# The router beside the last projection, expert weights through one ring, expert 0's rows put together on TensorE

## What is computed

```
mix = sigmoid(ga) * (o_a @ w_proj_a) + sigmoid(gb) * (o_b @ w_proj_b)
x   = x + mix @ w_out
h   = rms_norm(x, norm_ffn)
g      = argmax(h @ w_router_group + b)                      # one of 4 groups
top2   = top_k((h @ w_router_expert + b)[experts of g], 2)   # two of its 4 experts
weight = softmax(top2 values) * softmax(group logits)[g]
x   = x + sum over the two experts e of weight_e * ((silu(h @ w_gate[e]) * (h @ w_up[e])) @ w_down[e])
y   = rms_norm(x, norm_final)
```

## Time and profile before

| | us |
|---|---|
| Runs | 1137.81, 1140.47, 1141.32 (median 1140.47) |
| Profiled execution | 1137.26, span 1135.3, mean PE clock 0.950 |
| PE busy | 1022.2 (90%) |
| DVE, ACT, POOL busy | 642.3, 540.9, 141.9 |
| pb's last product to wo's first | 685.82 to 689.25 |
| First expert product | 795.97 |
| Last product of the last down projection | 1097.24 |
| First gathered output row added (DVE) | 1111.91 |

### The profile page before, as it was taken

How to read it: one execution, slowest core, us unless ns; L and a number is a source line. 1 busy time by engine, 2 the same in 40 slices (tenths; PEclk the granted TensorE clock), 3 DMA queues, 4 the chain that set the end, 5 groups by cost and what they waited for, 6 DMA issues and landing times.

```text
span 1135.3 us, 17498 instructions
## 1 busy us (share of the span) xinstructions
PE 1022.2 (90%) x7174; PEld 933.4 (82%) x7174; DVE 642.3 (57%) x919; ACT 540.9 (48%) x717; POOL 141.9 (13%) x138
## 2 busy tenths in 40 slices
PE   2999999999999999999899898981799999999940
PEld 2999999998999988888888898971688888888830
DVE  5233731344221267686665464247488988989826
ACT  6215633342222245454645422061478778887722
POOL 3300000000000123332211100022001010110003
PEclk8999999999999999999999999985799999999975
DMA  7863545417465375574434446123689999999726
GB/s 158 259 85 72 55 76 69 82 39 111 73 76 111 62 115 64 72 78 82 151 115 131 147 146 256 51 95 114 204 308 414 414 413 414 413 414 414 272 113 236
DMA packets 125514, 198.01 MB, mean 174 GB/s; under 512 B 10864, under 2 KB 72304, under 8 KB 125440
## 3 DMA queue, kind: packets, MB, share of 16 engines
q1 hardware_dynamic: 112336, 149.37, 49.4%
q0 software_dynamic: 10176, 36.97, 8.9%
q10 hardware_dynamic: 2928, 10.62, 2.3%
HBM read 174.40 MB, written 22.54 MB: 173 GB/s over the span
## 4 chain that ended last, share of the span: by engine, by line
PE 84%; DVE 6%; DMA 4%; ACT 3%; issue 2%; POOL 0%; ACTq 0%; DVEq 0%; POOLq 0%
PE ps L1019 24%; PE ps L1021 23%; PE ps L1020 23%; PE ps L1004 5%; DMA ring<-in_w_in_dram 2%; PE ps L1153 2%; PE ps L1139 2%; DVE x L1767 1%; DVE h_lo L1371 1%; PE ps L1083 1%; PE ps L1115 1%; PE ps L1099 1%; PE ps L1114 1%; DVE fo L1762 1%; DMA yg<-y_rows,ysl 1%
## 5 line engine op out<-in xcount | busy, mean ns | idle before, releaser
L1704 DVE TENSOR_TENSOR e_lo<-raw,e_hi 128x2048 fp32r<-128x2048 f32 x94 | 215.0, 2289 | 48.1 <-ACT e_hi L906 47.7
L906 ACT ACTIVATE e_hi<-raw 128x2048 fp32r<-128x2048 f32 x96 | 184.2, 1918 | 70.2 <-PE ps L1021 53.1
L1019 PE MATMUL ps<-h_hi,w_hi 128*128 128x272 f32 x640 | 189.9, 297 | 3.9 <-DVE h_lo L1371 3.9
L1021 PE MATMUL ps<-h_hi,w_lo 128*128 128x272 f32 x640 | 185.6, 290 | 0.0
L1020 PE MATMUL ps<-h_lo,w_hi 128*128 128x272 f32 x640 | 185.1, 289 | 0.0
L1382 DVE TENSOR_TENSOR w_lo<-ring,w_hi 128x2048 fp32r<-128x2048 f32 (+1 forms) x44 | 81.7, 1856 | 107.8 <-ACT w_hi L708 107.8
L708 ACT ACTIVATE w_hi<-ring 128x1024 fp32r<-128x1024 f32 (+1 forms) x60 | 87.2, 1453 | 107.4 <-PE ps L1021 98.5
L1019 PE MATMUL ps<-w_hi,h_hi 128*128 128x256 f32 x480 | 136.4, 284 | 0.0
L1020 PE MATMUL ps<-w_lo,h_hi 128*128 128x256 f32 x480 | 135.7, 283 | 0.0
L1021 PE MATMUL ps<-w_hi,h_lo 128*128 128x256 f32 x480 | 134.8, 281 | 0.0
L1019 PEld LDWEIGHTS ps<-h_hi,w_hi 128*128 128x128 f32 x640 | 121.5, 190 | 5.1 <-DVE h_lo L1371 4.1
(11 more groups left out here) (349 smaller groups left out, 2006.3 us busy)
## 6 DMA issues: line engine op xcount, KB each, us to landing
raw<-in_w_gate_dram SPq DMA_DIRECT2D x32, 1024.0 KB, 10.7
raw<-in_w_up_dram SPq DMA_DIRECT2D x32, 1024.0 KB, 11.0
raw<-in_w_down_dram SPq DMA_DIRECT2D x32, 1024.0 KB, 9.7
ring<-in_w_in_dram SPq DMA_DIRECT2D x24, 1024.0 KB, 9.3
ring<-in_w_in_dram SPq DMA_DIRECT2D x16, 512.0 KB, 8.4
y_rows<-yo ACTq DMA_DIRECT2D x16, 512.0 KB, 6.0
y_rows<-att POOLq DMA_DIRECT2D x8, 512.0 KB, 13.7
kraw<-in_cache_k_dram POOLq DMA_DIRECT2D x8, 512.0 KB, 5.3
```

The costliest lines, as they stand in the source:

```text
L906: act.activation(e_hi[:, buf], raw[:, slot], ACT.Copy).then_inc(s_ehi, 1)
L1019: pe.matmul(out, left[0], right[0], start=first, stop=False)
L1021: return pe.matmul(out, left[1], right[0], start=False, stop=final)
L1704: dve.tensor_tensor(e_lo[:, buf], raw[:, slot], e_hi[:, buf].bitcast(F32), ALU.subtract).then_inc(s_elo, 1)
```

## The change

*wo by token tile.* w_out comes in four quarters (512 rows x 512 columns, 1 MB each). They lie in places 6, 8, 10 and 11 of the experts' ring, which has twelve places now. SP issues the first two ahead of proj_b's fourth tile, the other two after pb. Their splits (wo_apart) stand behind pb units 5 and 9 and wo units 0 and 1. A wo unit is one token tile x 512 columns, 24 products, in the order WO_ORDER; the first waits for pb's chunks one by one.

*Router by token tile.* As soon as both halves of a token tile are added to x2, PE turns x2 itself (not h2) and makes its logits, with the norm's gains multiplied into the router's weights at the start and 1/rms applied after. DVE's route and slots follow for that tile alone. POOL then scatters h2's rows by index to x_rows, which has 640 rows for each expert, so an expert's rows lie together. x_rows is zeroed early in the run (17 writes; y_rows' 8 as before).

*Expert 0.* Tiles 0 to 2 reach expert 0 by way of x_rows (xg_first); the rows of tiles 3 and 4 are added on PE by products with one-hot matrices (into). Later experts' rows come by a plain DMA (block_in).

*Experts' weights.* SP's loads are written out and wait only for PE to have used the part that lay in the place twelve parts before; e_lo is written over raw. POOL makes no e_lo.

*Overflow and weights last.* The overflow blocks, the place of each token's output rows and the weights of the two experts are worked out on DVE behind the last hh_lo.

```diff
+WO_ORDER = [(0, 0), (1, 0), (2, 0), (0, 1), (1, 1), (2, 1), (3, 0), (3, 1), (4, 0), (4, 1)]
...
+        for k, u in enumerate((pb[5], pb[9], wo[0], wo[1])):
+            hook(u, "wo_apart", k)
...
+        dve_hooks = {wo[3]: [("h2", 0), ("route", 0)], wo[4]: [("h2", 1), ("slots", 0), ("route", 1)],
+                     wo[5]: [("h2", 2), ("slots", 1), ("route", 2)], wo[6]: [("slots", 2), ("early", 0)],
+                     wo[7]: [("h2", 3), ("route", 3)], wo[8]: [("slots", 3)],
+                     wo[9]: [("root", 4), ("route", 4), ("h2", 4), ("slots", 4)]}
...
+                if n == first_pb + 3:
+                    sp.wait_ge(s_oblo, 6)
+                    load_wo(0)
+                    load_wo(1)
...
-                if n == first_wo:
-                    sp.wait_ge(s_oblo, 6)
...
+            emptied(sp, pb[-1])
+            load_wo(2)
+            load_wo(3)
...
+            for seq, (e, j) in enumerate(in_order):
+                if seq == 5:
+                    sp.wait_ge(s_unit, wo[8] + 1)
+                elif seq == 9:
+                    sp.wait_ge(s_unit, wo[9] + 1)
+                    sp.wait_ge(s_xg[0], 16)
+                elif seq >= RAW:
+                    sp.wait_ge(s_part, seq - RAW + 1)
+                load_part(e, j, seq % RAW)
...
+            def rows_out(i):
                 n = TILES[i][1]
                 pool.wait_ge(s_h2, i + 1)
+                pool.wait_ge(s_slot, i + 1)
+                for k in range(2):
+                    pool.indirect_dma_start(x_rows, bass.IndirectOffsetOnAxis(slot_i[0:n, k, i:i + 1], 0), h2[i % 2][0:n],
+                                            None).then_inc(s_sc[i % 2], 16)
+            def block_in(e):
+                pool.dma_start(xg[:, e % 2], x_rows[ROWS * e:ROWS * e + CAP]).then_inc(s_xg[e % 2], 16)
+            for i in range(NTILE - 2):
+                rows_out(i)
+            pool.wait_ge(s_sc[0], 64)
+            pool.wait_ge(s_sc[1], 32)
+            pool.wait_ge(s_unit, wo[7] + 1)
+            pool.dma_start(xg_first, x_rows[0:CAP].rearrange("p (c n) -> p c n", c=KC // 2)).then_inc(s_xg[0], 16)
+            pool.wait_ge(s_xg[0], 16)
+            for i in range(NTILE - 2, NTILE):
+                rows_out(i)
+            pool.wait_ge(s_sc[0], 96)
+            pool.wait_ge(s_sc[1], 64)
+            block_in(1)
...
-            for j in range(2):
-                seq, buf, slot, _ = part_of(0, j)
-                pool.wait_ge(s_ehi, seq + 1)
-                pool.tensor_tensor(e_lo[:, buf], raw[:, slot], e_hi[:, buf].bitcast(F32), ALU.subtract).then_inc(s_elo, 1)
-            pool.wait_ge(s_slot, 1)
...
+                    for c in range(KC):
+                        k, cols = 2 * b + c // 4, slice(512 * (c % 4), 512 * (c % 4) + 512)
+                        if u == wo[0]:
+                            for m in pb[2 * c:2 * c + 2]:
+                                emptied(pe, m)
+                        last = three_products(ps[:, bank], (m_hi[:, c, toks], m_lo[:, c, toks]), (wo_hi[k][:, cols], e_lo[WO_RAW[k]][:, cols]),
+                                              c == 0, c == KC - 1)
+                        for what in inside.get((u, c), []):
+                            do(*what)
...
-            XT(0, 0, 16)
+            pe.wait_ge(s_xg[0], 16)
+            for c in range(KC):
+                out, cols = ps[:, 4 + c // 4, P * (c % 4):P * (c % 4) + P], slice(P * c, P * c + P)
+                pe.matmul(out, xg_first[:, c // 2, P * (c % 2):P * (c % 2) + P], ident[:], start=True, stop=False)
+                if c == 0:
+                    pe.wait_ge(s_h2, NTILE - 1)
+                    pe.wait_ge(s_into, 1)
+                pe.matmul(out, h2[1][:, cols], into[:, 0], start=False, stop=False)
+                if c == 0:
+                    pe.wait_ge(s_h2, NTILE)
+                    pe.wait_ge(s_into, 2)
+                last = pe.matmul(out, h2[0][0:TS, cols], into[0:TS, 1], start=False, stop=True)
+            last.then_inc(s_xt, 1)
...
                     if i >= 2:
-                        dve.wait_ge(s_h2st[i % 2], 16 * (i // 2))
-                        dve.wait_ge(s_h2x, i - 1)
+                        dve.wait_ge(s_sc[i % 2], 32 * (i // 2))
...
+            def route(i, n):
+                dve.wait_ge(s_lgm, i + 1)
+                step(dve.scalar_tensor_tensor(lg[0:n, i], ps[0:n, 5 + i % 2, 0:NG + NE], stat[0:n, 45 + i:46 + i], br[0:n], ALU.mult, ALU.add))
...
+                step(dve.max(best[0:n, i], masked))
+                step(dve.max_index(which[0:n], best[0:n, i], masked))
...
+            def slots(i, n):
+                dve.wait_ge(s_rank, i + 1)
...
+                dve.tensor_copy(slot_i[0:n, :, i], slot_f[0:n, :, i]).then_inc(s_slot, 1)
...
             body(NE - 1, 1, last=True)
             h_out(NE - 1)
+            overflow()
+            weights()
```

More of the change, by code:

```diff
@@ L87, in layout_of_units @@
                 add("AD"[h % 2], tile=None, kind="ox", nth=h, a=0, b=0, first=False, last=False, token_major=False)
+    first_wo = len(tiles)
+    for half in range(2):
+        for c in range(0, KC, KC // 2):
+            tiles.append(("w_out", c, KC // 2, half * D // 2, D // 2))
+            kinds.append("wo")
+    for i, half in WO_ORDER:
+        add("D", tile=first_wo + 2 * half, kind="wo", nth=half, a=i, b=half, first=False, last=False, token_major=False)
     return tiles, kinds, units
@@ L218, in build @@
[L218 to L226, removed]
-        lg = at("lg", AT_X, [P, NTILE, NG + NE])
@@ new lines, in build @@
+        xg = at("xg", AT_H + 8192, [P, 2, D])
+        x_hi = at("x_hi", AT_H + 16384, [P, 2, KC, P], F32R)
+        x_lo = at("x_lo", AT_H + 24576, [P, 2, KC, P], F32R)
+        hh_hi = at("hh_hi", AT_H + 32768, [P, FE // P, P], F32R)
+        hh_lo = at("hh_lo", 189440, [P, FE // P, P], F32R)
+        hh = at("hh", 151552, [P, 2, FE])
+        sg = at("sg", 116736, [P, FE])
+        yo = at("yo", AT_SA, [P, 2, D])
+        lg = at("lg", AT_X, [P, NTILE, NG + NE])
+        iota_e = at("iota_e", AT_X + 416, [P, NE])
@@ L674, in _ @@
+            block_in(1)
+            pool.dma_start(gfin[:], norm_final.unsqueeze(0).broadcast_to([P, D])).then_inc(s_gf, 16)
+            for e in range(2, NE):
+                pool.wait_ge(s_xt, e - 1)
+                block_in(e)
             pool.wait_ge(s_ovi, 1)
@@ L837, in squares, with part_hi @@
+            def part_hi(part):
+                if part:
+                    seq, buf, slot, loads = part
+                    act.wait_ge(s_raw[slot], loads)
+                    after(act, s_part, seq - (PBUF - 1))
+                    act.activation(e_hi[buf][:], raw[slot][:], ACT.Copy).then_inc(s_ehi, 1)
             def squares(h):
@@ L936, in y_out @@
                 act.wait_ge(s_y, e + 1)
[L937 to L940 removed]
+                act.dma_start(y_rows[bass.ds(e * CAP, CAP)], yo[:, slot]).then_inc(s_yst[slot], 16)
             def store_count(e, slot):
@@ L1285, in Dn @@
                         w = slice(D * i + 512 * b, D * i + 512 * b + 512)
-                        last = three_products(ps[:, 6 + b], (hh_hi[:, c], hh_lo[:, c]), (e_hi[:, buf, w], e_lo[:, buf, w]),
+                        last = three_products(ps[:, 6 + b], (hh_hi[:, c], hh_lo[:, c]), (e_hi[buf][:, w], e_lo[low][:, w]),
                                               c == 0, c == FE // P - 1)
@@ L1510, in head_rows, with part_lo @@
+            def part_lo(part):
+                if part:
+                    seq, buf, slot, _ = part
+                    dve.wait_ge(s_ehi, len(WO_RAW) + seq + 1)
+                    dve.tensor_tensor(e_lo[slot][:], raw[slot][:], e_hi[buf][:].bitcast(F32), ALU.subtract).then_inc(s_elo, 1)
             def head_rows(h):
@@ L1604, in _ @@
                             dve.tensor_copy(dst, src).then_inc(s_ev["D"], 1)
-                if d["last"] and d["tile"] + RING < len(wtiles):
+                if d["last"] and d["tile"] + RING < first_wo:
                     take_apart(d["tile"] + RING)
-                for what in hooks.get(u, []):
+                for what in dve_hooks.get(u, hooks.get(u, [])):
                     do(*what)
-            def t3d(k, n):
-                return rt[:, k, 0:NTILE * n].rearrange("p (i e) -> p i e", e=n)
@@ L1693, in _ @@
-            step(dve.tensor_reduce(ovb[:], ovm[:, :, 1], AX_X, ALU.add))
-            step(dve.tensor_copy(ovi[:, 1:1 + NOVF], ovb[:]))
-            dve.tensor_copy(ovi[:, 0:1], ov[:, 3, NE - 1:NE]).then_inc(s_ovi, 1)
-            dve.wait_ge(s_ovi, 1)
-            def part_lo(part):
-                if part:
-                    seq, buf, slot, _ = part
-                    dve.wait_ge(s_ehi, seq + 1)
-                    dve.tensor_tensor(e_lo[:, buf], raw[:, slot], e_hi[:, buf].bitcast(F32), ALU.subtract).then_inc(s_elo, 1)
+            part_lo(part_of(0, 1))
```

621 lines of the change are left out of this document (337 added, 284 removed).

## The result

| | before | after |
|---|---|---|
| Median (us) | 1140.17, 4 runs, 1137.81 to 1141.32 | 1128.30, 4 runs, 1128.02 to 1129.16 |
| Profiled execution; its span; clock | 1137.26; 1135.3; 0.950 | 1128.53; 1126.7; 0.962 |
| First expert product | 795.97 | 791.50 |
| First product of the last down projection | 1090.13 | 1081.53 |
| From there to the end of the span | 45.2 | 45.2 |

The ratio is 0.9905 (0.989 to 0.9921): faster by 11.9 us. The forecast was 1111, a gain of 29, in a range of 1101 to 1122. The direction was right; the size and the range were wrong. Between the two profiled executions the gain is 8.7: 4.5 until the first expert, 4.1 in the tail, nothing in between and nothing behind. The forecast had 22.5 and 5.1. So the question is where 18 us between pb and the first expert went.

A forecast was written before the change was run, and what follows sets the result against it. The prediction took PE to bound the kernel (84% of the chain of waits), with the router as target. It summed -22.5 to the first expert and -5.1 in the tail to -27.6: 1109.7, plus 1.3 gives 1111 us, range 1101 to 1122.

The forecast's parts named there:

- So I price them at 0.246 each, 5.9: Ahead of the first expert: 24 products putting expert 0's rows together, priced from slow router transposes at 5.9 us.
- The wo stage, 65.5 forecast: wo stage: 54.7 us for 240 products, plus x2 transposes 4.7, logits 5.1 and rank products 1.0.
- pb's end, 692 forecast: pb stage: ends at 692, 2 us later for two w_out splits and 4 for the late fourth proj_b tile.
- The route from wo's end to the first product behind it: After wo: tile 4's eviction, turn and logits 2.2 us, route 3.5, rank and slots 2; products start 7.7 after.
- The wait for w_down: Tail: w_down halves loaded well ahead, 7.0 us before the last down projection becomes 3.8, gain 3.2.
- the nine products should run at 0.228: Last down projection: no wait as long as the harmless 3.14 us, so nine slow products speed up, gain 1.9 us.
- scatters were not waited for by h2(2) and h2(3): wo stage: DVE waits for scatters before reusing h2 buffers; landing taken as 5 us, no cost.
- the overflow steps were covered: Tail: 43 overflow, slot and weight steps behind the last hh_lo on DVE; cost 0, at worst +3 us.
- rival C: Crowded DMA, 13%: fourth proj_b tile lands past 660, pb ends at 697, second expert's rows late; +8, 1119 us.
- B: Everything early, 15%: w_out and fourth proj_b tile first, pb ends at 688, 24 products and first expert full pace; 1102 us.
- D: Scatters that wait, 5%: three landings one behind the other; whole gain gone from 16.5 us each, 1149 us at 20.
- E: Nothing in the sum, 4%: first expert starts earlier but the expert loop waits for weights by as much; 1136 to 1142 us.

The follow-up runs named there:

- e3: Changed kernel with 16 idle identity products in PE's four waits for tile 4's routing, the 24 real products unchanged: 1121.59 us, ratio 0.9844.
- e1: Changed kernel with expert 0's 24 products replaced by 8 plain transposes, leaving out the rows of tiles 3 and 4: 1115.53 us, ratio 0.9788.
- e2: Changed kernel with 16 of the 24 products moved earlier, into PE's four waits for tile 4's routing: 1117.49 us, ratio 0.9816.
- e4: Changed kernel with the first two w_out quarters loaded behind proj_b's fifth and sixth tiles, their splits behind pb units 9 and 13: 1120.64 us, ratio 0.983.
- e7: Changed kernel with 6 idle products between the last transposes and the last down projection: 1127.25 us, ratio 0.9895 to the kernel before.
- e6: Changed kernel with 16 products earlier, later w_out loads, idle products in three PE waits, and turns and logits one chunk later in wo: 1107.35 us.
- e5: Changed kernel with both the 16 earlier products and the later w_out loads: 1112.28 us, ratio 0.9752 to the kernel before.
- e8: Changed kernel with expert 0's rows by DMA: scatter of all five tiles, plain read, 8 transposes, no one-hot products: 1123.30 us, ratio 0.9861.

## Why the prediction was wrong

Between pb and the first expert the forecast had -22.5 and the traces show -4.5. 17.6 of the 18.0 us, step by step:

- **"So I price them at 0.246 each, 5.9"** is the step that failed: 9.1 us. The row it came from the earlier trace rows is of transposes; the 24 are sums of float32 products, which PE does as two instructions each. The rows I had chosen showed it: 756.50 has "x32" for what the instruction list has as 16 products. At the lower clock a chunk of three takes 1.85 us, at the upper 1.03 (e3). Two instructions each at 0.246 would make 11.8 us; the other 3.2 are there because an instruction of a sum took 0.313 at the lower clock where a transpose takes 0.246, and why no run shows. e1 takes the products away and gets 12.8 back. The Trainium skill, "FP8 and Floating Point Precision", section "TensorE Precision Notes", says that true float32 takes four passes through the PE array; the trace agrees in kind only: 0.29 us for 128 columns at the upper clock (e2), where by the earlier trace rows a quarter of a 512-column split product, at 0.228, is 0.057, so a factor of five, and two instructions and not four.
- **The wo stage, 65.5 forecast, 70.5 measured** (695.54 to about 766): 5.0 us. The same misreading: the row at 756.50 counts 32 instructions for 16 products, so logits took 1.70 a tile and not 1.14 (+1.6 in all, as the last half tile's came behind the stage). Waits of PE for evictions, 0.83 and 0.77 (+1.6), which I had left out: the eviction stands behind a route on DVE. The 240 products at 0.238 and not 0.228 (+2.4). The turns took less (-1.1), the ranks 0.2 more.
- **pb's end, 692 forecast, 695.5 measured.** Of the 3.5 us, 2.3 were there when pb began (642.28 against 639.96 for the last of ob_lo): 0.8 from the start of the run, and 1.5 from a wait of 2.35 us near 613, behind which PE kept its upper clock in before's execution and lost it for some 3 us in after's (the lines are at the end). The change does nothing there, and this may be why the medians are 11.9 apart and the two profiled executions 8.7. The other 1.2 is a balance: the fourth proj_b tile was usable some 3 us later than I had it even so, the products behind it ran at the low clock until 666, and the 2 us for the two splits were not needed. e4 shows what the order of the loads cost: with them moved and the splits still in the stage, 7.7 us go.
- **The route from wo's end to the first product behind it** (768 to 774) was as forecast, and so were the x_hi, x_lo and the slow first ten.

In the tail the forecast was -5.1 and -4.1 was measured. The wait for w_down went as it should (7.0 us to 3.1, 0.7 better than forecast). But **"the nine products should run at 0.228"** failed: with a wait of 2.54 us PE still lost its clock, not at once but after four products (0.63 from 1082.83). e7 and e6 fill the wait and the clock stays. That 3.14 us were harmless once was one row; near 613 a wait of 2.35 us cost the clock in one execution and not in the other, so in these traces the length of a wait alone doesn't tell.

What held: nothing was lost in the expert loop, scatters were not waited for by h2(2) and h2(3) (ACT is what DVE waits for there), and the overflow steps were covered: in after their flag is written by 1087.85, 2.1 us ahead of ACT's last store. Of rival C the first half nearly came (the tile reached ACT at 660.23, pb ended at 695.5), the second did not: the second expert's rows were not late in after. B, D and E missed. None of the rivals priced the products.

## What to carry to other kernels

Compare the count of a group in the trace with the count in the program before taking a duration "of one": a float32 product on TensorE is two instructions here and 0.29 to 0.35 us for 128 columns at the upper clock (e2, e3), while a transpose of the same size is 0.13, so a price taken from transposes says nothing about a sum of products. Work that a late piece does not need belongs in the waits ahead of it, where it cost nothing here (16 of 24 products moved: 10.8 us); in e2's trace it also held the clock, in e5's the clock fell all the same. A load put ahead in a queue delays all that stands behind it: its price is read at the first tile behind it that an engine needs, not at its own use.

## What the runs showed of the hardware

- POOL's indirect DMA takes 0.95 us to issue, but 2.26 when it starts inside a long DVE subtraction (749.30 to 751.58), and the same again at 774.32 (2.23). From the timeline of all engines of after:

```profile
749.30 2.28 DVE L1667 TENSOR_TENSOR e_lo<-raw,e_hi 128x2048 fp32r<-128x2048 f32 x1
...
750.14 2.26 POOL L707 DMA_INDIRECT x_rows<-h,slot_i  x1 [5.60 <-DVE slot_i L1660]
752.71 0.95 POOL L707 DMA_INDIRECT x_rows<-h,slot_i  x1 [0.30 <-issue]
...
774.32 2.23 POOL L707 DMA_INDIRECT x_rows<-h,slot_i  x1 [7.40 <-DVE slot_i L1660]
```

  That is the rule of the Trainium skill, "SBUF — State Buffer", section "SBUF: two separate sides", that I weighed: here the trace agrees, with 1.3 us a time. In after nothing was behind it that PE waited for; in e8 the first of tile 4's two scatters (2.23 us at 772.02) stood on the way to the first expert.
- PE's clock can fall after PE is busy again: four products at the upper level, the last three at 0.23 each, then seven at 0.43 with a mixed one on either side (after, 1081.53 to 1086.16; granted clock 1.00 in 1081.5 to 1082.5, 0.50 in 1082.8 to 1085.8).
- The same wait can cost the clock in one execution and not in another. PE's timeline behind a wait of 2.35 us, which the change does not touch, first in before, then in after (granted clock 1.00 in 613.2 to 618 of before, 0.50 in 615.0 to 618.4 of after):

```profile
613.23 0.39 PE L1019 MATMUL ps<-oa_hi,w_hi 128*128 128x272 f32 x1 [2.35 <-ACT qbT L882]
...
615.10 0.29 PE L1021 MATMUL ps<-oa_hi,w_lo 128*128 128x272 f32 x1
...
614.03 0.39 PE L1090 MATMUL ps<-oa_hi,w_hi 128*128 128x272 f32 x1 [2.35 <-ACT qbT L970]
...
615.69 0.43 PE L1091 MATMUL ps<-oa_lo,w_hi 128*128 128x272 f32 x1
```

- Sixteen identity products in PE's waits, idle work, bought back 6.7 us (e3).
